# Moving eight pairs of modulation weights from the first layer's attention turns to the second layer's

## The reference

```
sh1, sc1, g1, sh2, sc2, g2 = split(silu(cond) @ w_ada[l] + b_ada[l], 6)   # w_ada[l]: 1024 x 6144
h    = rms_norm(x, norm1_g) * (1 + sc1) + sh1
proj = h @ w_in            # latents of attention, convolution input, q/k/v of neighbourhood attention
mix  = concat(o_mla (8 heads), o_conv (256 channels, 31 taps), o_na (4 heads))
x    = x + g1 * (mix @ w_out)
h    = rms_norm(x, norm2_g) * (1 + sc2) + sh2
x    = x + g2 * grouped_moe(h)          # 16 experts, top 2 of one group of 4
```

## Time and profile before

| | us |
|---|---|
| median of three runs | 1277.75 |
| the profiled execution, its own time | 1276.07 |
| its span in the profile | 1274.0 |
| TensorE matmul busy | 1107.8 (87%) |
| VectorE busy | 863.5 (68%) |
| ScalarE busy | 651.1 (51%) |
| GpSimd busy | 216.8 (17%) |
| ring loads | 276.59 MB |
| whole traffic, mean | 248 GB/s |

### The profile page before, as it was taken

One profiled execution on the slowest core, in us unless ns is written; L12 is line 12 of the kernel. 1 busy time (PEld: TensorE's weight loads), 2 busy tenths in 40 slices (PEclk: granted clock), 3 DMA queues, 4 the chain that ended last, 5 costly groups with the idle time before them and its releaser, 6 DMA issues.

```text
span 1274.0 us, 15531 instructions
## 1 busy us (share of the span) xinstructions
PE 1107.8 (87%) x5994; PEld 903.6 (71%) x5994; DVE 863.5 (68%) x1063; ACT 651.1 (51%) x884; POOL 216.8 (17%) x197
## 2 busy tenths in 40 slices
PE   5899989989599999999827998788959999999980
PEld 2787757778478888888727876568847888888860
DVE  1138187533679999889641667871379999998943
ACT  2212244431277888888622114452237888888841
POOL 5001111000204111221003021110022311221100
PEclk9999998969799999999968997797969999999995
DMA  9865785720589999999742321011358999999923
GB/s 358 282 234 209 292 327 199 279 94 21 189 335 374 369 379 387 381 379 378 304 161 80 119 75 67 0 44 66 126 215 318 383 382 372 372 372 387 375 75 154
DMA packets 54155, 315.75 MB, mean 248 GB/s; under 512 B 11920, under 2 KB 12032, under 8 KB 19648
## 3 DMA queue, kind: packets, MB, share of 16 engines
q1 hardware_dynamic: 38448, 276.59, 56.9%
q0 software_dynamic: 14000, 31.85, 6.9%
q10 hardware_dynamic: 1632, 6.29, 1.3%
HBM read 313.40 MB, written 22.30 MB: 263 GB/s over the span
## 4 chain that ended last, share of the span: by engine, by line
PE 74%; DVE 15%; DMA 5%; issue 3%; ACT 2%; POOL 1%; SPq 0%; POOLq 0%; DVEq 0%; ACTq 0%
PE bank L1015 42%; PE bank L732 10%; PE bank L933 6%; PE bank L721 3%; DMA ring<-wring_dram 3%; DVE conv_acc L1729 3%; PE bank L1007 2%; PE bank L838 2%; PE bank L810 2%; PE bank L743 1%; PE bank L824 1%; DVE rowmax L1540 1%; PE bank L776 1%; PE bank L753 1%; PE bank L1044 1%
## 5 line engine op out<-in xcount | busy, mean ns | idle before, releaser
L1936 DVE TENSOR_TENSOR w_lo<-ring,w_hi 128x2048 fp32r<-128x2048 f32 x192 | 436.4, 2288 | 58.5 <-ACT w_hi L1286 58.3
L1286 ACT CAST w_hi<-ring 128x2048 fp32r<-128x2048 f32 x192 | 367.2, 1917 | 32.6 <-PE bank L1015 32.4
L1015 PE MATMUL bank<-w_hi,hgT_hi 128*128 128x512 f32 x512 | 204.6, 400 | 5.2 <-issue 3.3
L1015 PE MATMUL bank<-w_hi,hgT_lo 128*128 128x512 f32 x512 | 201.4, 393 | 0.0
L1015 PE MATMUL bank<-w_lo,hgT_hi 128*128 128x512 f32 x512 | 200.9, 392 | 0.0
L732 PE MATMUL bank<-ring,hT 128*128 128x256 f32 (+1 forms) x672 | 139.6, 368 | 2.3 <-DVE hT L1428 2.3
L732 PEld LDWEIGHTS bank<-ring,hT 128*128 128x128 f32 x672 | 122.0, 190 | 18.6 <-DVE hT L1428 2.8
L671 POOL DMA_INDIRECT y_rows<-y,y_at x32 | 48.7, 1521 | 448.1 <-ACT y L1316 434.3
L1015 PEld LDWEIGHTS bank<-w_hi,hgT_hi 128*128 128x128 f32 x512 | 97.2, 190 | 26.4 <-issue 7.2
L1015 PE MATMUL bank<-w_hi,hidT_hi 128*128 128x512 f32 x256 | 104.1, 407 | 9.9 <-DVE hidT_lo L1958 9.9
L1015 PEld LDWEIGHTS bank<-w_hi,hgT_lo 128*128 128x128 f32 x512 | 96.9, 189 | 21.0
(11 more groups left out here) (241 smaller groups left out, 1479.8 us busy)
## 6 DMA issues: line engine op xcount, KB each, us to landing
ring<-wring_dram SPq DMA_DIRECT2D x260, 1024.0 KB, 7.9
parts<-y_rows ACTq DMA_DIRECT2D x6, 1024.0 KB, 7.1
kT<-mod_dram POOLq DMA_DIRECT2D x4, 1024.0 KB, 8.8
ring<-wring_dram SPq DMA_DIRECT2D x6, 640.0 KB, 4.3
h_rows<-h_tok POOLq DMA_DIRECT2D x6, 512.0 KB, 3.0
bias<-na_bias_dram POOLq DMA_DIRECT2D x32, 64.0 KB, 4.8
A<-mod_dram POOLq DMA_DIRECT2D x2, 1024.0 KB, 4.9
SH<-mod_dram POOLq DMA_DIRECT2D x2, 1024.0 KB, 6.8
```

What stands on the lines that cost most here:

```text
L1015: mm = pe.matmul(b[:, :], a, w[m], start=(start and k == 0), stop=(stop and k == 2))
L1286: act.copy(w_hi[:, q, :], in_ring(l, expert_slot(e, i))).then_inc(hi_made[q], 1)
L1936: dve.tensor_tensor(w_lo[:, q, :], in_ring(l, expert_slot(e, i)), w_hi[:, q, :], ALU.subtract) \
```

## The change

The pairs of layer 1 are split. Pairs 0 to 3 of layer 1 are still taken in layer 0 (two before the heads, one at the end of turn 0, one at the end of turn 1). Pairs 4 to 11 of layer 1 are taken at the end of turns 0 to 7 of layer 1's own attention. The last open pair is closed at the end of turn 8, in both layers. The bias and the gain are made in turn 9 and the rows transposed in turn 10, in both layers. `mod_rows` lies in `conv_in` instead of `biased`, so VectorE's wait for the store goes; GpSimd's store of the keys and the root for the convolution stand ahead of the rows' store and the load of G.

```diff
-LATER_PAIRS = [(0, k) for k in range(4, PAIRS)] + [(n, k) for n in range(1, DEPTH) for k in range(PAIRS)]
+LATER_PAIRS = [[(n, k) for k in range(4, PAIRS)] + [(n + 1, k) for k in range(4) if n + 1 < DEPTH] for n in range(DEPTH)]
+TAKEN_IN = {p: 0 for p in FIRST_PAIRS}
+TAKEN_IN.update({p: n for n in range(DEPTH) for p in LATER_PAIRS[n]})
 def pairs_after(n, what, i=0):
-    if n:
+    if n and what != "turn":
         return []
-    first = {"proj": i, "heads": AMONG_PROJ, "turn": AMONG_PROJ + BEFORE_HEADS + i}[what]
+    first = i if n else {"proj": i, "heads": AMONG_PROJ, "turn": AMONG_PROJ + BEFORE_HEADS + i}[what]
-    return LATER_PAIRS[first:first + count]
+    return LATER_PAIRS[n][first:first + count]
+MODS_DONE, ROWS_TURNED = 8, 10
...
-        mod_rows = biased[0:4 * 2 * KC, 0, 0, 0:P]
+        mod_rows = conv_in[0:4 * 2 * KC, 0, C_CTX:C_CTX + P]
...
                 # GpSimd: now ahead of the rows' store and the load of G
+                pool.wait_ge(sems["heads_normed"], nth(l, "heads_normed", 3))
+                pool.dma_start(new_nak[n]..., qk[:, 3, :, 0:NAD])
+                root(l, "conv", TILES)
...
                 # TensorE, ScalarE: rows transposed and copied at i == ROWS_TURNED, no longer at i == 3
-                close_modulation(l)
+                    if i == MODS_DONE:
+                        close_modulation(l)
...
-                        if (g, t) == (8, 1):
-                            dve.wait_ge(sems["rows_stored"], nth(l, "rows_stored", 16))
...
-                    if i == 1:
-                        if n == 0:
-                            dve.wait_ge(*once_read(l, ("mod", 0, PAIRS - 1)))
-                            ada_bias(l, 0, 2, 2)
-                            dve.wait_ge(mods_made, 2)
+                    if i == MODS_DONE + 1:
+                        dve.wait_ge(*once_read(l, ("mod", *LATER_PAIRS[n][-1])))
+                        ada_bias(l, n, 2, 2)
+                        if n + 1 < DEPTH:
+                            ada_bias(l, n + 1, 2, 1)
+                        dve.wait_ge(mods_made, 3 if n == 0 else 4)
                         gain(l, modT[:, n, 4, :, :], V_N2, 4, 2)
...
-                if n == 0:
-                    dve.wait_ge(*once_read(l, ("mod", *LATER_PAIRS[-1])))
-                    for m in range(1, DEPTH):
-                        ada_bias(l, m, 0, 2)
-                    dve.wait_ge(mods_made, DEPTH + 1)
```

More of the change, by code:

```diff
@@ L185, in psum_plan @@
         if i == 3:
-            order += heads_transposed(1) + [("rows",)]
+            order += heads_transposed(1)
         if i == 7:
@@ L192, in psum_plan @@
             order += [("ln", 0), ("ln", 1)]
+        if i == ROWS_TURNED:
+            order += [("rows",)]
         pairs(pairs_after(n, "turn", i))
-    order += [("mod", *p) for p in open_pair]
+        if i == MODS_DONE:
+            order += [("mod", *p) for p in open_pair]
+            open_pair.clear()
     order += [("mix", c) for c in range(6)]
@@ L247 @@
 Layer = namedtuple("Layer", "n")
-ADA_PASS = Layer(0)
 def build(nc, wring, x_in, vec, rows, ckv_cache, kr_cache, nak_cache, nav_cache, cond, w_router,
@@ L463, in left @@
             if s < S_IN:
-                return once_full(ADA_PASS, ("ada", n, s))
+                return once_full(Layer(TAKEN_IN[n, s // 2]), ("ada", n, s))
             if s < S_UP:
@@ L617, in _ @@
                     .then_inc(sems["na_cache_loaded"], 16)
+                pool.wait_ge(sems["heads_normed"], nth(l, "heads_normed", 3))
+                pool.dma_start(new_nak[n].rearrange("p (h n) -> p h n", h=NAH), qk[:, 3, :, 0:NAD]) \
+                    .then_inc(sems["keys_stored"], 16)
+                root(l, "conv", TILES)
                 pool.wait_ge(*once_read(l, ("rows",)))
@@ L624, in _ @@
                 pool.dma_start(G, mod_dram[n][0].partition_broadcast(P)).then_inc(sems["gate1_loaded"], 16)
[L625 to L628, removed]
                 pool.wait_ge(sems["na_exp_done"], nth(l, "na_exp_done", 2 * 4))
@@ L899, in _ @@
                         turn_heads(l, 1)
[L901 to L905, removed]
                     if i == 7:
@@ L917, in _ @@
                             turn_around(l, ("ln", c), [ln_tm[:, t, c * P:(c + 1) * P] for t in range(TILES)])
+                    if i == ROWS_TURNED:
+                        pe.wait_ge(sems["mod_ready"], nth(l, "mod_ready", 2))
+                        pe.wait_ge(*once_free(l, ("rows",)))
+                        pe.transpose(bank[bank_no(l, ("rows",))][0:4 * 2 * KC, 0:P],
+                                     modT[:, n, 2:6, :, :].rearrange("p m q c -> p (m q c)"), iden[:]) \
+                          .then_inc(bank_full[bank_no(l, ("rows",))], 1)
                     modulation(l, pairs_after(n, "turn", i))
-                close_modulation(l)
+                    if i == MODS_DONE:
+                        close_modulation(l)
                 pe.wait_ge(*once_read(l, ("O", len(GROUPS) - 1)))
@@ L1265, in _ @@
                         evac_turned(l, 1)
+                    if i == 7:
+                        evac_turned(l, 2)
+                    if i == ROWS_TURNED:
                         act.wait_ge(*once_full(l, ("rows",)))
@@ L1268, in _ @@
                             .then_inc(bank_read[bank_no(l, ("rows",))], 1)
-                    if i == 7:
-                        evac_turned(l, 2)
                     evac_modulation(l, pairs_after(n, "turn", i))
-                close_modulation(l)
+                    if i == MODS_DONE:
+                        close_modulation(l)
                 for c in range(6):
```

## The result

The changed kernel took 1284.05 us (median of six runs, 1280.61 to 1285.97), the kernel before in the same comparison 1279.02 us. The ratio is 1.004, with an interval from 1.0024 to 1.0055: slower by 5 us where 1.1 us less was forecast. The prediction calls anything under 0.5% "no change"; this is 0.4%, but it lies clear of the runs' scatter, on the other side, and 1 us beyond the range. As a difference, the 5.0 us lie just inside the bounds of the sum (-6.5 to +5.2): the kernel before was itself 1.3 us above its earlier median in this comparison.

A forecast was written before the change was run, and what follows sets the result against it. Expert stages were taken as bound by full-clock products, attention turns by hops between TensorE, ScalarE and VectorE. Layer 0's -12.1 and layer 1's +11.1 us sum to -1.1: 1276.6 us for the median, range 1269.5 to 1283.0.

The forecast's parts named there:

- Layer 0 and layer 1, pairs moved: Turns 0 to 8: layers swap patterns; layer 0 takes 38.84 + 28.58 us, layer 1 takes 41.60 + 35.85 us.
- Layer 0, turns 8 to 11: Layer 1's 17.58 us plus 0.98 for turning the last pair and 0.75 for VectorE's bias and gain: 19.31 us.
- the last one's turning: Layer 1, turns 8 to 11: turning stays, a pair's products (1.87 us) go, bias and gain add 0.45: 18.92 us.
- both ends of 14.42 us: Turn 11 to the start of mixing, in both layers: the time layer 1 took before, 14.42 us.
- the exchange comes to nothing: Attention turns of both layers: each borrowed duration carries its own granted clock, so swapping clocks between layers adds nothing.
- GpSimd's queue, loads, the rows: Both layers: G arrives with over seven microseconds of slack, ring loads and the rows' transposition in turn 10 cost nothing.
- (a): Rival: pairs fill TensorE's waits in layer 1's turns and cost 5.4 us there; 1271.0 us, chance 0.12.
- (d): Rival: the change only swaps the layers, every term cancels; 1277.75 us, chance 0.11.
- (b): Rival: pairs stop overlapping and cost layer 1 their full 22.8 us; 1288.4 us, decided from 18.5 us paid; chance 0.05.
- (c): Rival: G arrives over 7 us later than worked out, costing 1 us or two per layer; chance 0.02.
- signs of a wrong forecast: Layer 1's turns take under 107 or over 114 us, or anything outside the turns changes by over 2 us.
- One sign of a right one: Granted clock in layer 1's turns rises to 0.9, while layer 0's falls to about 0.8.

The follow-up runs named there:

- the wide products: Kernel before plus eight useless products of 256 columns and a copy at the end of layer 1's turn 8: 1277.16 us, ratio 1.0006.
- variant of one turn later: Changed kernel with layer 0's two pairs in turns 9 and 10, layer 1's in 3 to 10, closing in 11, rows in 12: 1282.81 us.
- The pair of runs: Kernel before plus, at the end of layer 1's turn 8, eight two-column products (1282.72 us) or products of 256 columns (1277.16 us).
- closing in turn 9: Changed kernel with all pairs in layer 0 as before, closed in turn 9, no closing in layer 1; bias, gain, rows late: 1284.0 us.
- the late variant: Changed kernel with layer 0's two pairs in turns 8 and 9, layer 1's in 2 to 9, closing in 10, rows in 11: 1276.5, then 1273.5 us.

## Why the prediction was wrong

**Layer 0 and layer 1, pairs moved.** Right in the mechanism. The comparison of the layers gave turns 0 to 8 within 0.6 us in the sum, with two misses in layer 1 that cancel, and with the waits that it named: pairs of turns 0 and 1 hidden behind VectorE, layer 1 taking over layer 0's pattern.

**Layer 0, turns 8 to 11: "Added are one turning of the last pair ... (0.98 us)".** This step failed, and the same one in layer 1 ("the last one's turning"), with both ends of 14.42 us behind it. Measured were 21.79 and 22.23 us instead of 19.31 and 18.92, and ends of 15.80 us. I priced the closing by its length and took the clock of the stretch as given by the rows that I borrowed. The length was right, as the wide products show (0.9 us). But the closing costs 4.47 + 1.38 = 5.9 us in layer 1 by the run that adds it alone, which is what the median of that run rose by within its interval (3.9 us, 2.4 to 6.9), and 3.3 us in layer 0 by the run that takes it away. The rest of the miss in layer 0 has its place in turn 10: even without the closing, turn 8 to mixing took 34.18 us where the sum had 17.58 + 0.75 + 14.42 = 32.75. Of the parts moved late, bias and gain were priced at 0.75 us and the rows at nothing; whether they bring the level down there is open.

**"Clock ... the exchange comes to nothing".** This is the same mistake as a rule. I treated the level as belonging to a layer's density of work. In layer 1's turn 8 the kind of products that TensorE had just made decided it. The rule that I set beside it (the Trainium skill, "TensorE: Matmul & The Clock Gate", "Part 1: The HAM clock gate") speaks of idling; here the level fell while TensorE had no wait at all for 6 us (busy 6.18 of 6.18), and it stayed down through the 16 us of full occupation that followed (16.05 of 16.05). So the rule as I used it doesn't cover this case, and the measurement decides.

**GpSimd's queue, loads, the rows.** Right for the queue and the loads: no wait of TensorE on the ring in layer 1's turns, and G in time. For the rows' transposition, priced at nothing, the medians show no cost and the profiles leave it open.

**The rivals.** (a) and (d) didn't come. (b) had the right sign and the wrong mechanism: layer 1 paid 15.3 us, not over 18.5, and not because pairs stopped overlapping. (c) didn't come. No rival of mine was one in which the clock falls at a place where it had not fallen before.

**The signs and the range.** Both signs of a wrong forecast came: layer 1 took 115.05 us, over 114, and the stretch before turn 0 changed by 3.36 us (below). One sign of a right one didn't: the clock of layer 1's turns was 0.79, the same as before, not up to 0.9. The faster end of the range has a slip: 1271.2 less 2 is 1269.2, not 1269.5. It decides nothing.

**The profile against the median.** Turn 0 of layer 0 started 3.36 us later in the profile after. Ahead of it stand waits for the ring, 1.7 us in two in either profile, and there the level fell in this one. The same stretch before and after (windows):

```profile
154.00:157.50 3.50, 3.45 (x38) 2.87 (x39) 0.00 (x0) 1.36 (x5) 0.00 (x0) 1.00 1.01 421
```

```profile
154.00:157.50 3.50, 3.37 (x25) 2.39 (x26) 0.00 (x0) 0.00 (x0) 0.00 (x0) 0.58 0.99 414
```

In six of the fourteen profiles (the two kernels and the twelve runs) turn 0 started at 161.0 to 163.1 us, and these are the six in which this stretch had 0.50 to 0.58. In the other eight it had 1.00, and turn 0 started at 157.8 to 159.3. Both kinds occur with the moved pairs, and a late start came also in the wide-products kernel, which has none of the change. So it isn't the change's doing, and it is part of the kernel's scatter.

**What stays open.** Why the level fell behind the small products in layer 1 in each of the six profiles that have them in turn 7 or 8 without filler behind, but at changing places in layer 0; whether late bias and rows bring it down in turn 10; and why the variant of one turn later scatters by 16 us. The pair of runs shows that the kind of products decides it at that place; which of their properties, and what else has to stand around them, isn't known from these runs.

## What to carry to other kernels

Price a group of tiny products on TensorE not by its length but by what it may do to the clock of the stretch behind it: look where the granted clock stands at 1.0, and test the place with wide products of the same length. If small ones must be there, try wide work on both sides of them. That mostly helped here, not always (one turn later still); wide work just ahead alone did not save two sets of small ones in a row (closing in turn 9). When a comparison of like stretches is used as a price list, note the clock that each stretch had, and ask whether the edit would keep it.

## What was unexpected of the hardware

The level went from 1.0 to 0.5 behind eight products of two columns with TensorE occupied without a gap, and 16 us of uninterrupted transpositions (128 columns), scores (128 and 384) and value products (64) didn't bring it back (busy 16.05 of 16.05, clock 0.50). Useless wide work of 1.87 us per turn held it at 1.00. The same small products in pairs, with wide ones before and behind, mostly did no harm: turns 8 to 10 of the late variant ran at 1.00.
